# Gathering for eight experts at once in a two-layer mixture-of-experts kernel, with the last expert's weights in a fifth buffer

## What is computed

```python
scores = sigmoid(x @ w_router)                    # 64 experts
idx    = top 8 of (scores + e_bias), inside the 4 best of 8 groups
gates  = sel / sum(sel) * 2.5
routed = sum over chosen e: gate_e * (silu(x @ w_gate[e]) * (x @ w_up[e])) @ w_down[e]
x      = layer_norm(alpha * x + routed + shared(x))
```

## Time and profile before

| | |
|---|---|
| runs | 1419.1, 1419.69, 1415.24 us (median 1419.1) |
| profiled execution | 1414.79 us, of which the span from first to last instruction is 1412.9 us |
| TensorE busy | 1360.5 us, 96% of the span |
| VectorE, ScalarE busy | 434.0 us (31%), 268.4 us (19%) |
| DMA | 450.28 MB, mean 319 GB/s |
| expert loop of layer 0 | first `gate_up` at 143.6 us, last at 603.4 us |
| expert loop of layer 1 | first `gate_up` at 922.5 us, last at 1382.3 us |
| granted TensorE clock | 0.989 in the mean |

### The profile page before, as it was taken

How to read it: one execution, slowest core, us unless ns; L and a number is a source line. 1 busy time by engine, 2 the same in 40 slices (tenths; PEclk the granted TensorE clock), 3 DMA queues, 4 the chain that set the end, 5 groups by cost and what they waited for, 6 DMA issues and landing times.

```text
span 1412.9 us, 25031 instructions
## 1 busy us (share of the span) xinstructions
PE 1360.5 (96%) x10556; PEld 802.5 (57%) x10556; DVE 434.0 (31%) x967; ACT 268.4 (19%) x528; POOL 82.3 (6%) x114
## 2 busy tenths in 40 slices
PE   8979999999999999979999998999999999999996
PEld 7869444454444454436699997944444544445442
DVE  2244222222222222254553235522222222222224
ACT  1231211111111111112511433121111111111111
POOL 7202000000000000011004100200000000000000
PEclk9999999999999999989999999999999999999998
DMA  5686699999999999975232006569999999999992
GB/s 166 170 319 263 281 409 419 419 416 419 418 416 419 418 417 418 418 237 164 95 121 92 4 5 239 209 261 409 418 417 417 418 419 417 418 419 416 418 418 110
DMA packets 114448, 450.28 MB, mean 319 GB/s; under 512 B 15696, under 2 KB 45008, under 8 KB 81104
## 3 DMA queue, kind: packets, MB, share of 16 engines
q1 hardware_dynamic: 114384, 449.33, 79.8%
HBM read 448.26 MB, written 1.05 MB: 318 GB/s over the span
## 4 chain that ended last, share of the span: by engine, by line
PE 94%; DVE 3%; ACT 2%; issue 1%; DMA 0%; PEldq 0%; DVEq 0%; ACTq 0%
PE PS L1669 31%; PE PS L1695 16%; PE PS L1703 9%; PE PS L1647 8%; PE PS L460 4%; PE PS L1211 4%; PE PS L427 3%; PE PS L1770 2%; PE PS L1226 2%; PE PS L1340 2%; PE PS L1675 1%; PE PS L1359 1%; PE PS L1355 1%; PE PS L449 1%; PE PS L1325 1%
## 5 line engine op out<-in xcount | busy, mean ns | idle before, releaser
L1669 PE MATMUL PS<-RING,AR 128*64 128x512 f32 x1024 | 225.3, 592 | 1.9 <-issue 1.9
L1669 PE MATMUL PS<-AR 128*64 128x512 f32 x1024 | 225.2, 592 | 0.0
L1669 PEld LDWEIGHTS PS<-RING,AR 128*64 128x64 f32 x1024 | 74.3, 137 | 146.3 <-issue 146.3
L1669 PEld LDWEIGHTS PS<-AR 128*64 128x64 f32 x1024 | 73.9, 137 | 145.9 <-issue 145.8
L1978 DVE TENSOR_TENSOR y_parts<-PS,y_parts 128x512 fp32r<-128x512 f32 x128 | 88.5, 692 | 211.7 <-ACT y_parts L1897 211.7
L1955 DVE SCALAR_TENSOR_TENSOR AR<-AR,PS 128x256 f32<-128x256 f32 x64 | 30.7, 480 | 381.2 <-ACT AR L1875 381.2
L1703 PE MATMUL PS<-y_parts,token_map 128*128 128x512 f32 x496 | 146.4, 417 | 0.0
L1703 PEld LDWEIGHTS PS<-y_parts,token_map 128*128 128x128 f32 x496 | 83.5, 188 | 60.9 <-issue 50.3
L1695 PE MATMUL PS<-AR 128*64 128x512 f32 x512 | 116.9, 598 | 0.0
L1695 PE MATMUL PS<-RING,AR 128*64 128x512 f32 x512 | 116.9, 598 | 0.0
L1647 PE MATMUL PS<-slot_map,x_low 128*128 128x192 f32 x512 | 116.1, 273 | 0.0
(11 more groups left out here) (281 smaller groups left out, 1356.2 us busy)
## 6 DMA issues: line engine op xcount, KB each, us to landing
RING<-in_moe_w_gate SPq DMA_DIRECT2D x64, 1024.0 KB, 11.1
RING<-in_moe_w_up SPq DMA_DIRECT2D x64, 1024.0 KB, 13.2
RING<-in_moe_w_down SPq DMA_DIRECT2D x64, 1024.0 KB, 14.2
AR<-in_moe_w_gate SPq DMA_DIRECT2D x64, 1024.0 KB, 12.9
AR<-in_moe_w_up SPq DMA_DIRECT2D x64, 1024.0 KB, 15.0
AR<-in_moe_w_down SPq DMA_DIRECT2D x64, 1024.0 KB, 12.6
AR<-in_ab_w_in SPq DMA_DIRECT2D x8, 1024.0 KB, 5.8
AR<-in_rw_w_o SPq DMA_DIRECT2D x4, 1024.0 KB, 6.2
```

Source lines behind the costliest of these rows:

```text
L1669: ins = nc.tensor.matmul(PS[s * B:(s + 1) * B, 4, :], XG[:, k, c:c + B], gate_and_up(slots[s])[:, k, :, :], start=(k == 0), stop=(k == KT ...
```

## The change

The loop gathers for eight experts at once. A part of the gather is now one of eight chunks of x with 384 columns (8 experts x 48): 4 matmuls a part, 8 parts, once in four pairs. `SELR`, `SEL1` and `GQ` are made for eight experts, in the third pair of an oct; `SELR` has a semaphore of its own (`slots_ready`), and the parts are counted by four semaphores, for even and odd parts. The gathered x no longer fits in one place: chunks 0 to 3 go to `XGD`, which is laid over `xT` (the transposed x, dead once the shared expert and the router have read it), chunks 4 to 7 to `XGU` in `AR`. For that the area `XR` goes, the shared expert's SiLU is written to `HS` in place, and the pads are cleared in two steps. A fifth slot, `EX`, holds expert 63: gate and up over `flat[:, 0:4096]`, down over `GB`. It is loaded ahead of the loop, once `shared_gate_up` is there. The last pair then loads one expert. `load_ln` moves behind the last `down1`; in layer 0 the first two chunks of `w_key` move behind the last `gate_up`. Loop bodies are four pairs long and run 6 times (SyncE: two pairs, 14 times, with the last two pairs of loads written out).

```diff
         def wslot(s):
+            if s == EX:
+                return (flat[:, 0:2048].rearrange("p (k f) -> p k f", k=KT),
+                        flat[:, 2048:4096].rearrange("p (k f) -> p k f", k=KT),
+                        GB[:, :, :])
...
-        XG = am(KT, 4 * B)
-        XGS = XG.rearrange("p k (s b) -> p k s b", s=4)
+        XGU = am(KT // 2, 8 * B)
+        XGD = xT[:, :, :].rearrange("p k t -> p (k t)").rearrange("p (k f) -> p k f", k=KT // 2)
+
+        def gathered(k):
+            return (XGD, XGU)[k // 4][:, k % 4, :]
...
-                load_ln(sp, st)
-                with sp.Fori(1, PAIRS // 2) as i:
+                sp.wait_ge(q["shared_gate_up"], 1 + past["shared_gate_up"])
+                sp.wait_ge(s_ln, TT * st)
+                load_expert(sp, E - 1, EX)
...
+                with sp.Fori(1, PAIRS // 2 - 1) as i:
+                    load_pair(i, 0, (0, 1))
+                    load_pair(i, 1, (2, 3))
+                load_pair(PAIRS // 2 - 1, 0, (0, 1))
+                load_pair(PAIRS // 2 - 1, 1, (2,))
                 if l == 0:
-                    sp.wait_ge(q["shared_gate_up"], 1)
+                    sp.wait_ge(q["gate_up_done"], PAIRS)
                     for c in range(2):
                         load_rw(sp, w_key, c)
-                    sp.wait_ge(q["gate_up_done"], PAIRS)
+                sp.wait_ge(q["down1"], PAIRS + past["down1"])
+                load_ln(sp, st)
+                if l == 0:
                     for c in range(2, 4):
                         load_rw(sp, w_key, c)
...
             def gather(pe, part):
-                for k in range(2):
-                    for t in range(TT):
-                        for n in range(2):
-                            ins = nc.tensor.matmul(PS[:, 7 - part % 2, k * 4 * CAP:(k + 1) * 4 * CAP],
-                                                   XP[n][:, t, 2 * part + k, :],
+                for t in range(TT):
+                    for n in range(2):
+                        ins = nc.tensor.matmul(PS[:, 7 - part % 2, 0:8 * CAP], XP[n][:, t, part, :],
...
-                if half == 1 and more:
-                    for n in range(4):
+                if p == 3 and more:
+                    pe.wait_ge(q["slots_ready"], oct_ + 2 + past["slots_ready"])
+                    for n in range(KT):
                         if n >= 2:
-                            pe.wait_ge(q[f"gathered{n - 2}_copied"], use + 2 + past[f"gathered{n - 2}_copied"])
-                        gather(pe, n).then_inc(q[f"gathered{n}"], 1)
+                            wait_copied(pe, n - 2, oct_ + 1)
+                        gather(pe, n)
...
-                with pe.Fori(1, QUADS - 1) as i:
-                    pe_pair(pe, 2 * i, 0, False, True, False, i)
-                    pe_pair(pe, 2 * i + 1, 1, False, True, False, i)
+                with pe.Fori(1, OCTS - 1) as i:
+                    for p in range(4):
+                        pe_pair(pe, 4 * i + p, p, i, True)
...
-                if half == 0 and more:
-                    expert_gates(4 * use + 4, 4)
-                    onehot(4 * use + 4, 4, q["onehot_ready"])
+                if p == 2 and more:
+                    expert_gates(8 * oct_ + 8, 8)
+                    onehot(8 * oct_ + 8, 8, q["onehot_ready"], q["slots_ready"])
```

More of the change, by code:

```diff
@@ L34 @@
 PAIRS = E // 2
-QUADS = E // 4
+OCTS = E // 8
+EX = 4
 H0 = 8
@@ L1679, in moe_view, with turn_map @@
             map_bank = PS[:, 4, 256:384].bitcast(BF16)
[L1681 to L1683 removed]
+            def turn_map(pe, p):
+                sel = [SEL1[:, t, 2 * p:2 * p + 2, :].rearrange("p s b -> p (s b)") for t in range(TT)]
                 for t in range(TT):
@@ L1713, in shared_down, with pe_pair @@
                 return ins
-            def pe_pair(pe, i, half, first, more, last, use, opens=False):
-                slots = (2 * half, 2 * half + 1)
+            def pe_pair(pe, i, p, oct_, more, first=False, last=False, opens=False):
+                half = p % 2
+                slots = (2, EX) if last else (2 * half, 2 * half + 1)
                 if first:
                     pe.wait_ge(q["pads_cleared"], 1 + past["pads_cleared"])
-                if half == 0:
-                    for n in range(4):
-                        pe.wait_ge(q[f"gathered{n}_copied"], use + 1 + past[f"gathered{n}_copied"])
+                if p == 0:
+                    for n in range(KT - 2, KT):
+                        wait_copied(pe, n, oct_)
+                use = 0 if p < 2 else 1
                 for s in slots:
-                    pe.wait_ge(q["gu_w"][s], 32 * use + 32 + past["gu_w"])
+                    pe.wait_ge(q["gu_w"][s], 32 * (l * uses[s] + 1) if s == EX else
+                               64 * oct_ + 32 * (l * uses[s] + use + 1))
                 pe.wait_ge(q["map_copied"], i + 1 + past["map_copied"])
                 pe.wait_ge(q["gates_ready"], i + 1 + past["gates_ready"])
-                gate_up(pe, slots, half).then_inc(q["gate_up_done"], 1)
+                gate_up(pe, slots, p).then_inc(q["gate_up_done"], 1)
                 if first:
@@ L1889, in act_pair @@
                     s.wait_ge(q["scattered"], i + past["scattered"])
-                    copy_map(s, 1 - half)
-                if half == 1 and more:
-                    for n in (1, 3):
-                        s.wait_ge(q[f"gathered{n}"], use + 2 + past[f"gathered{n}"])
-                        copy_gathered(nc.scalar.copy, n).then_inc(q[f"gathered{n}_copied"], 1)
+                    copy_map(s, 1 - p % 2)
+                if p == 3 and more:
+                    for n in range(1, KT, 2):
+                        wait_gathered(s, n, oct_ + 1)
+                        copy_gathered(nc.scalar.copy, n).then_inc(q["odd_copied"], 1)
                 for h in range(2):
@@ L1959, in copy_hidden, with dve_pair @@
                 return nc.vector.tensor_copy(HT[:, :, :].rearrange("p f b -> p (f b)"), PS[:, 4, 0:FT * 2 * B])
-            def dve_pair(v, i, half, more, last, use):
+            def dve_pair(v, i, p, oct_, more, last=False):
+                half = p % 2
                 v.wait_ge(q["silu_ready"], i + 1 + past["silu_ready"])
```

182 lines of the change are left out of this document (96 added, 86 removed).

## The result

The changed kernel runs in 1424.96 us, median of 11 runs (1421.79 to 1429.73); the kernel before, on the same chip, in 1418.4. One of the kernel before's 11 runs took 2184.61 us and stands in no ratio. The ratio of all the others is 1.0054, with a 95% interval of 1.0039 to 1.0069: the medians lie 6.6 us apart, and the ratio amounts to 7.7 us (5.5 to 9.8). The changed kernel is slower, clear of the noise, where the forecast was +1.1 us and so no change.

A forecast was written before the change was run, and what follows sets the result against it. TensorE and the weight queue were taken to finish together, the queue deciding after the change. Loop -3.2 and -2.5, norm waits +3.5 and +3.3: +1.1 us on the profiled 1414.8, so 1415.9, about 1420 as median; range 1408 to 1431.

The forecast's parts named there:

- Queue and TensorE finish together: Expert loop before the change: both end together, with 0.9 us of room in layer 0 and 0.25 in layer 1.
- The gather: In the loop: 6.2 us in place of 7.1, 0.9 saved an oct; 7 gathers a layer, 6.3 us off TensorE's path.
- The head: Ahead of pair 0: eight gather parts cost +2.3 us, maps and stalls 0.3; +2.6 us a layer in sum.
- The queue decides, by half a microsecond to one: Last `gate_up`: weights allow 600.2 and 1379.8, TensorE alone 599.7 and 1378.6; gain 3.2 and 2.5 us.
- two loads fewer: Weight queue at the last `gate_up`: the load awaited is the 176th, not the 178th, 5.0 us less.
- landings well ahead of their `gate_up`: Sign of being wrong: the queue's last landings come well before the `gate_up` that needs them; no size given.
- Behind the last pair: The layer norm waits for parameters loaded after the last `down1`: 3.5 us in layer 0, 3.3 in layer 1.
- Code stalls: Rival, loop on TensorE: the long body waits for a code fetch each turn, 15.6 us a layer; 1450, chance 0.13.
- Dear columns: Rival, gather: 384 columns cost 0.23 us a matmul, 7.8 for 7.1 with stalls; 1441, chance 0.07.
- The queue gives way: Rival, weight queue: 418 GB/s is only TensorE's demand, gather 5.3 us, 12.6 saved a layer; 1406, chance 0.10.
- Parameters in time: Rival, layer norm: its parameters arrive without a wait, -5.7 us in all; 1413, chance 0.07.
- the main case: Whole kernel: queue decides and norm waits; chance 0.55, own range 1414 to 1425, mostly no change.

The follow-up runs named there:

- before_light: The kernel before with the loop's down loads cut to a quarter of each matrix (output differs, totals not compared): loops 459.78 and 459.77 us, 1471.42 us in all.
- after_light: The changed kernel with the loop's down loads cut to a quarter of each matrix (output differs, totals not compared): 1464.97 us, ratio 1.0332.
- octs_alone: The changed kernel without the fifth buffer: expert 63 through slot 3, norm parameters loaded ahead of the loop; 1419.88 us, ratio 1.0014 to the kernel before.
- down_in_slot3: The changed kernel with expert 63's down matrix in slot 3, `GB` free and `load_ln` ahead of the loop: 1417.61 us, ratio 1.0002 to the kernel before.
- before_ln_late: The kernel before with only `load_ln` moved, behind the last `down1`: 1426.12 us, ratio 1.0061 to the kernel before.
- expert7: The changed kernel with expert 7 instead of 63 in the fifth buffer, norm parameters issued behind the last weights: 1418.92 us, ratio 1.0014 to the kernel before.
- busy kernels: Useless matmuls in TensorE's idle time before layer 1's mixer, added to expert31, the kernel before and before_ln_late: 1416.14, 1426.37, 1435.15 us; with fewer, on expert31, 1409.1.
- expert31: As expert7, but with expert 31, which pair 15 uses, in the fifth buffer: 1411.68 us, ratio 0.9959 to the kernel before.
- before_busy: The kernel before with 85 useless matmuls on TensorE between the transposes of the norm's output: 1426.37 us, ratio 1.006 to the kernel before.

## Why the prediction was right or wrong

**Queue and TensorE finish together: right for before.** before_light shows it from TensorE's side (459.78 us with the queue relieved, 459.77 without), and every saving on TensorE alone did run into the queue.

**The gather: right in price, wrong in count.** 32 matmuls of 384 columns take 6.28 us, forecast 6.2. Two neighbours lie 0.18 apart, as the straight line said (timeline of TensorE in after), and the rest is stalls for copies:

```profile
375.31 0.34 PE L1663 MATMUL PS<-slot_map,x_high 128*128 128x384 f32 x1
375.49 0.35 PE L1663 MATMUL PS<-slot_map,x_low 128*128 128x384 f32 x1
```

A full oct is 58.50 in place of 2 x 29.67 = 59.33, -0.83, forecast -0.9. But the prediction counted "7 gathers inside the loop", 6.3 us. The kernel before has 15 gathers between the first and the last `gate_up`, after has 7: 15 x 3.55 - 7 x 6.28 = 9.3, and the two light kernels differ by 9.5. The head's +2.3 was charged for the larger first gather, and the quad's gather that it makes needless was never credited. TensorE alone would have its last `gate_up` at 596.8 (after_light), not at 599.7. This miscount alone moves nothing in the forecast's sum, since that took the queue's time in both layers.

**The head: right.** +2.75 us a layer, forecast +2.6.

**The step that failed: "The queue decides, by half a microsecond to one".** The queue does decide, but the comparison was made at one place, the last `gate_up`, and that is the wrong one. With the count mended, TensorE is ahead of the queue by much more than that half microsecond, and it meets it early and in every oct: three pairs without a gather take 13.04 us each (364.81 less 351.77 is one), their six loads 15.06, and only the pair with the gather lets the queue catch up. So the last place where weights bind is pair 27, and up to there the change takes nothing out of the queue: expert 63's loads stand behind it. In layer 0 the last `gate_up` is 546.17 + 58.69 = 604.86. Of the forecast 5.0 us for two loads fewer the queue did deliver its part (the last up matrix landed at 601.3; with the forecast's 600.05 and a start of the router 2.07 us later, 602.1 was forecast), but TensorE had still 3.5 us of its own work: landings well ahead of their `gate_up` are what the prediction named as a sign of being wrong. What the fifth buffer saves is the pause at pair 31, some 1.5 us a layer, as octs_alone shows. The loop's gain is 3.33 and 2.92 in place of 5.8 and 5.1: 4.7 of the 5.5 us that were missing in the sum.

**Behind the last pair: right in mechanism, a little small in layer 0.** The waits are +4.42 and +2.89, forecast 3.5 and 3.3; in layer 0 the bias took 6.5 us with two chunks of `w_key` ahead of it, just above its bound of 4.3 (its own +9 and 4 make 4.5). down_in_slot3 removes both waits and with them the loss.

**The rivals.** *Code stalls*: refuted. The Trainium skill, Runtime: NRT & Kernel Launch, Instruction fetch mechanics, says that a taken branch to a target outside a window of two 16 KiB pages stalls for a fetch, and gives TensorE 128 KiB. By the first the body of 568 instructions would stall in each turn; between 255 and 560 us the trace holds no code packet, so the measurement goes with the second. *Dear columns*: refuted, 6.28 us. *The queue gives way*: refuted, 418 GB/s in the octs where TensorE waits. *Parameters in time*: refuted, the norm waits in both layers. The outcome was none of them, but the main case with a term of the loop mis-sized; at 1424.96 it is at the very edge of that case's own range. That it fell inside owes something to luck: the loop's term was wrong by 4.7 us, and bounds made for other terms took it in.

**What stays open.** The stages of the MoE account for 6.6 us, which is the difference of the medians. The two profiled executions differ by 14. Of the rest the longest part is the mixer of layer 1, 283.26 us in after for 278.00 in before, at a lower mean clock. 1.4 us of it is in the window shown above and goes with the norm's wait: before_ln_late, with the wait alone, has it too (34.1 us). But kernels without the wait took 33.1 to 33.9 there, and a second stretch later in that mixer was long (14.1 us for 12.5) in after and before_ln_late, but also in expert7, which has no wait, and in most of the busy kernels; it was short (10.8) in octs_alone and down_in_slot3. Single profiles don't settle this. The granted clock that is on record for every run does settle one half: it is 0.9845 in the mean of after's 11 runs and 0.9844 in the 7 of before_ln_late, against 0.9878 in the 61 runs of the kernel before beside the experiments, and 0.9872 to 0.9885 in octs_alone, down_in_slot3, expert7 and expert31. So the norm's wait does go with a lower clock. What that costs is not told apart from the noise: about 1 us in each (means 7.6 us above before for 6.6 by the stages in after, 7.8 for 6.8 in before_ln_late, 8.6 by its median). What sets the length of each slow stretch stays open.

## What to carry to other kernels

Where an engine and a transfer queue run at nearly the same pace, compare them at every point where one may wait for the other, not at the end alone: work that is unevenly spread (one large gather in four pairs) lets the engine run into the queue once in each period, even where the sums for the whole loop are equal. A spare buffer is worth its loads only if they leave the queue ahead of the place where it binds and behind the place where it runs dry; the same buffer was worth some 1.5 us a layer with the last expert, 5.4 with the one in the middle, and next to nothing with an early one. Before a buffer is laid over "dead" data, look at who needs that data next: a load of 1 MiB of parameters that had always been early cost more than the buffer brought.

## What the runs showed of the hardware

- A matmul of 384 columns of this type costs 6.28 / 32 = 0.196 us with the stalls for its copies, against 0.111 for 192. Without the stalls two of them lie 0.18 apart, which is the straight line between 192 and 512.
- A loop body of 568 TensorE instructions ran in layer 0 from 255 us, in its first turn, to 560 us, in its last, without one code packet.
- Two loads that write 128 copies of a row of 4 KB (512 KB each) took 5.0 and 5.1 us from the second one's issue to landing with nothing else in the queue (layer 1 of before_ln_late and after), 6.0 with two loads behind them (layer 0 of before_ln_late), and 6.5 with two ahead and two behind (layer 0 of after).
- A float32 matmul of 128 columns appears as two instructions, 0.114 to 0.116 us each (7.98 / 70 and 4.18 / 36 in before_busy).
- A pause costs 0.2 us more than the profile shows as idle. Between two matmuls without a pause the second starts 0.17 us before the first one's modelled end, and that overlap is lost; and a `gate_up` takes 7.09 us from its first start to its last end after a pause, 7.04 without one (the 6.87 of the chain leaves the 0.17 out), at a granted clock of 1.00 in both. The four pauses of a layer make 0.9 of the 1 us by which TensorE's busy time in after (451.28) lies above that of after_light (450.27).
